# The first input projection of a two-block layer: values, gates and both z products in pairs of column chunks with seven block products in place of eight

## The reference

```python
h = rms_norm(x, norm_g)
proj = jnp.einsum('bsd,dn->bsn', h, w_in)
(q_a, k_a, v_a, o_a, i_a, f_a, z_a, c_q, c_kv, k_r, z_b, g_a, g_b) = jnp.split(proj, offsets, axis=-1)
...
y_a = jnp.einsum('bsc,cd->bsd', jax.nn.sigmoid(o_a) * h_a * jax.nn.silu(z_a), w_a)
...
y_b = jnp.einsum('bsc,cd->bsd', o_b * jax.nn.silu(z_b), w_b)
```

## Time and profile before

| | |
|---|---|
| median of 3 runs | 2136.06 us (2136.01 to 2136.29) |
| the profiled execution | 2135.79 us |
| its span, first to last instruction | 2133.6 us |
| PE busy | 2111.0 us, 99% |
| DVE busy | 1317.1 us, 62% |
| ACT busy | 1052.0 us, 49% |
| mean granted clock of PE | 0.999 of full speed |

### The profile page before, as it was taken

The page is one execution under the profiler, slowest core; times in us unless marked ns, Lnnn a source line. Parts: engine busy times, 40 slices in busy tenths (PEclk is TensorE's granted clock), DMA queues, the critical chain, the costliest instruction groups (busy, mean ns, idle before and its releaser), DMA issues.

```text
span 2133.6 us, 25857 instructions
## 1 busy us (share of the span) xinstructions
PE 2111.0 (99%) x10130; PEld 1764.8 (83%) x10130; DVE 1317.1 (62%) x1675; ACT 1052.0 (49%) x1344; POOL 37.8 (2%) x49
## 2 busy tenths in 40 slices
PE   8999999999999999999999999999999999999998
PEld 7888888888888877788888888888888888888886
DVE  5874454555555776556554455456786787687675
ACT  6445454445444675454445444354544544454443
POOL 0000000000000020000000000000000000000000
PEclk9999999999999999999999999999999999999999
DMA  7455555564465544355755442455555455555453
GB/s 268 178 191 189 193 195 197 192 227 177 174 225 197 188 152 147 135 217 197 293 187 185 180 172 103 151 185 198 182 212 194 180 199 199 189 187 215 178 197 119
DMA packets 56550, 402.44 MB, mean 189 GB/s; under 512 B 6240, under 2 KB 6496, under 8 KB 9216
## 3 DMA queue, kind: packets, MB, share of 16 engines
q1 hardware_dynamic: 53648, 380.67, 49.5%
q0 software_dynamic: 2656, 19.81, 2.4%
q10 hardware_dynamic: 144, 0.52, 0.1%
HBM read 392.59 MB, written 8.39 MB: 188 GB/s over the span
## 4 chain that ended last, share of the span: by engine, by line
PE 97%; ACT 1%; issue 1%; DVE 0%; DMA 0%; SPq 0%; POOLq 0%; POOL 0%; DVEq 0%; ACTq 0%
PE proj L554 20%; PE proj L556 20%; PE proj L555 20%; PE proj L929 11%; PE proj L932 6%; PE proj L964 2%; PE proj L965 2%; PE tbank L530 2%; PE proj L963 2%; PE tbank L963 1%; PE tbank L964 1%; PE tbank L965 1%; PE bank_a L965 1%; PE bank_a L963 1%; PE bank_a L964 1%; PE bank_a L731 1%
## 5 line engine op out<-in xcount | busy, mean ns | idle before, releaser
L1554 DVE TENSOR_TENSOR w_lo<-raw,w_hi 128x1024 fp32r<-128x1024 f32 x714 | 861.5, 1214 | 717.8 <-ACT w_hi L1092 709.5
L1092 ACT ACTIVATE w_hi<-raw 128x1024 fp32r<-128x1024 f32 x714 | 748.5, 1052 | 958.7 <-PE proj L556 663.4
L554 PE MATMUL proj<-w_hi,a_both 128*128 128x512 f32 x1728 | 686.5, 397 | 0.0
L556 PE MATMUL proj<-w_hi,a_both 128*128 128x512 f32 x1728 | 674.1, 390 | 0.0
L555 PE MATMUL proj<-w_lo,a_both 128*128 128x512 f32 x1728 | 672.7, 389 | 0.0
L556 PEld LDWEIGHTS proj<-w_hi,a_both 128*128 128x128 f32 x1728 | 324.3, 188 | 69.2
L554 PEld LDWEIGHTS proj<-w_hi,a_both 128*128 128x128 f32 x1728 | 324.5, 188 | 68.5 <-issue 4.3
L555 PEld LDWEIGHTS proj<-w_lo,a_both 128*128 128x128 f32 x1728 | 324.8, 188 | 65.1
L929 PE MATMUL proj<-a_both,w_hi 128*128 128x512 f32 x1024 | 256.5, 392 | 0.3 <-DVE a_both L1597 0.3
L929 PEld LDWEIGHTS proj<-a_both,w_hi 128*128 128x128 f32 x1024 | 184.4, 189 | 33.7 <-DVE a_both L1597 0.5
L932 PEld LDWEIGHTS proj<-a_both,w_lo 128*128 128x128 f32 x1024 | 139.7, 190 | 10.0
(11 more groups left out here) (376 smaller groups left out, 1823.1 us busy)
## 6 DMA issues: line engine op xcount, KB each, us to landing
raw<-stream SPq DMA_DIRECT2D x359, 1024.0 KB, 4.8
nat<-x SPq DMA_DIRECT2D x4, 512.0 KB, 8.2
z_store<-z POOLq DMA_DIRECT2D x1, 2048.0 KB, 8.3
ga_store<-z POOLq DMA_DIRECT2D x1, 2048.0 KB, 12.5
gb_store<-z POOLq DMA_DIRECT2D x4, 512.0 KB, 7.1
yb<-z_store POOLq DMA_DIRECT2D x4, 512.0 KB, 6.8
ga<-ga_store POOLq DMA_DIRECT2D x1, 2048.0 KB, 8.2
gb<-gb_store POOLq DMA_DIRECT2D x1, 2048.0 KB, 14.5
```

Source lines behind the costliest of these rows:

```text
L554: nc.tensor.matmul(banks[t][:, :], ah, wh, start=first, stop=False)
L556: last = nc.tensor.matmul(banks[t][:, :], al, wh, start=False, stop=end)
L1092: A((w_hi_end if extra else w_hi)[:, piece.n % RING, 0:width], src, ACT.Copy).then_inc(w_rounded, 1)
L1554: V.tensor_tensor(lo[:, s, 0:width], src, hi[:, s, 0:width].bitcast(f32), SUB).then_inc(w_rest, 1)
```

## The change

The 16 chunks of v, o, z_a and z_b become eight pairs (`PAIRS_IN`): two of v, four of one o and one z_a chunk each, two of z_b. Pairs 1 to 7 have their two sum steps where the MLP has them, pair 0 at steps 3 and 5, with the contraction tiles put in another order, so that the sums of the left side (`xs`, made once, in the k chunks, by `sum_x`, `round_x_sums` and `rest_of_x_sums`) serve all eight pairs. The mixed banks go through a buffer in SBUF, `joined`: `join_mixed` combines them after the second sum step, `join_whole` adds the whole banks at the end of the pair and leaves the finished chunks in `joined`, and what ACT and DVE do with the chunks (`take_v`, `take_o`, `take_z`) stands in the first step of the pair that follows and reads `joined`, where it read the banks. The convolution of the last k chunk, the angles of the rotation and `rope_k` are put in slots of pairs 0 and 1 (`side`). The loops are written out, on SyncE too. The helpers of the MLP's pairs are used for both.

```diff
+UNITS_IN = 1 + 4 * 4
+PAIRS_IN = 8
+SUM_AT_IN = [(3, 5)] + [SUM_AT] * (PAIRS_IN - 1)
+ORDER_IN = [(0, 2, 3, 1, 5, 4, 6, 7)] + [tuple(range(STEPS))] * (PAIRS_IN - 1)
...
+        parts_in = ([proj[2], proj[3], proj[0], proj[1]], [bank_a, bank_b] + tbank)
...
+            def pair_in(p):
+
+                whole, mixed = parts_in[p % 2], parts_in[1 - p % 2]
+                at = SUM_AT_IN[p]
+                if p:
+                    pe.wait_ge(part_read, 5 * (p - 1) + 1)
+                else:
+                    pe.wait_ge(proj_read, chunk.at() * 2)
+                for step in range(STEPS):
+                    kt = 2 * ORDER_IN[p][step]
+                    if step == at[0]:
+                        if p:
+                            pe.wait_ge(part_read, 5 * p)
+                        else:
+                            pe.wait_ge(m_sum, 1)
+                            pe.wait_ge(t_by_dve, by_dve.at())
+                    if step in at:
+                        i = at.index(step)
+                        sum_step(kt, whole, mixed, a_hi, a_lo, xs_hi[:, i], xs_lo[:, i], i + 1, i == 0, i == len(at) - 1)
...
+            def round_x_sums(i):
+
+                act.wait_ge(ms_summed, i + 1)
+                A(xs_hi[:, i, :, :], xs[:, :, :], ACT.Copy).then_inc(ms_rounded, 1)
+
+            def k_slot(j, i):
+                conv_slot(j)
+                if i in (2, 3) and j == 7:
+                    round_x_sums(i - 2)
...
+            def take_o(p, n):
+
+                act.wait_ge(whole_added, 4 * (p + 1))
+                for t in range(TT):
+                    if n == 0:
+                        act.wait_ge(gated, tiles.at(2))
+                        A(stg[:, t, :], joined[:, 2 * t, :], ACT.Sigmoid, scale=inv1[:, t:t + 1]).then_inc(proj_read, 1)
+                    else:
+                        A(stg2[:, t, :], joined[:, 2 * t + 1, :], ACT.Sigmoid, scale=inv1[:, t:t + 1]).then_inc(sig, 1)
...
+            def take_o(n):
+
+                if n == 0:
+                    return
+                i = tiles.n // 2
+                for t in range(TT):
+                    tiles.add()
+                    dve.wait_ge(sig, tiles.at())
+                    chain(V.tensor_tensor(stg2[:, t, :], stg2[:, t, :], stg[:, t, :], MUL))
+                    V.scalar_tensor_tensor(nat[:, t, i * CW:(i + 1) * CW], joined[:, 2 * t + 1, :], inv1[:, t:t + 1],
+                                           stg2[:, t, :], MUL, MUL).then_inc(gated, 1)
...
+            def join_mixed(p, part):
+
+                mixed, m = parts_in[1 - p % 2], joined
+                if part == 0:
+                    if p in (1, 2):
+                        dve.wait_ge(proj_read, chunk.at() * 2)
+                    dve.wait_ge(m_copied, p + 1)
+                    chain(V.tensor_tensor(m[:, 2, :], mixed[2][:, :], m[:, 0, :], ADD))
+                    V.tensor_tensor(m[:, 1, :], mixed[1][:, :], m[:, 2, :], ADD).then_inc(dve_seq, 1)
+                    seq.add()
+                else:
+                    chain(V.tensor_tensor(m[:, 2, :], mixed[3][:, :], m[:, 2, :], ADD))
+                    V.tensor_tensor(m[:, 3, :], mixed[1][:, :], m[:, 2, :], ADD).then_inc(part_read, 1)
...
+            def side(p, js):
+
+                if p == 0:
+                    conv_slot(js, 3)
+                    if js == 0:
+                        rest_of_x_sums(1)
+                    if js in (9, 13):
+                        if js == 9:
+                            dve.wait_ge(early_ready, 16)
+                        angles((js - 9) // 4)
+                if p == 1 and js == 6:
+                    rope_k()
+
+            def pair_in(p):
+
+                at = SUM_AT_IN[p]
+                for step in range(STEPS):
+                    def slot(j):
+                        if step in at:
+                            if j % 2 == 0:
+                                side(p, 2 * step + j // 2)
+                        else:
+                            side(p, 2 * step + j)
+                        if step == 0:
+                            take(p - 1, j)
+                        if step == at[-1] + 1:
+                            join_mixed(p, j)
+                    if step == STEPS - 1:
+                        join_whole(p)
+                    pieces(4 if step in at else 2, slot=slot)
+                chunk.add(2)
```

More of the change, by code:

```diff
@@ L655, in _, with product @@
                 project(a_hi, a_lo, slot=lambda j: stg_slot(j, i, at=(1, 3)))
[L657 to L665, removed]
+            def product(bank, hi, lo, wh, wl, first=False, end=False):
+                nc.tensor.matmul(bank[:, :], hi, wh, start=first, stop=False)
+                nc.tensor.matmul(bank[:, :], hi, wl, start=False, stop=False)
+                return nc.tensor.matmul(bank[:, :], lo, wh, start=False, stop=end)
@@ new lines, in weights, with plain_step @@
+            def weights(ahead, half):
+                s = (piece.n + ahead) % RING
+                cols = slice(half * CW, (half + 1) * CW)
+                return w_hi[:, s, cols], w_lo[:, s, cols]
+            def plain_step(kt, whole, hi, lo, first=False, slot=None):
+                for h in range(2):
+                    pe.wait_ge(w_rest, piece.at(1))
+                    for t in range(TT):
+                        tok = slice(t * P, (t + 1) * P)
+                        for n in range(2):
+                            last = product(whole[2 * t + n], hi[:, kt + h, tok], lo[:, kt + h, tok],
+                                           *weights(0, n), first=first and h == 0)
+                    last.then_inc(w_used, 1)
+                    piece.add()
+                    if slot:
+                        slot(h)
@@ L959, in project_last @@
                 chunk.add()
[L961 to L983, removed]
@@ L1189, in _, with trig_slot @@
-            act.wait_ge(proj_read, chunk.at() * 2)
-            act.sem_inc(v_ready, 8)
-            tiles = Tally()
-            with loop(act, 4, {piece: 16, done: 16, chunk: 2, tiles: 2}) as i:
-                pieces()
-                for t, b in enumerate(banks()):
+            def trig_slot(j):
+                if j == 4:
+                    act.wait_ge(trig_arg, 2)
+                    A(sin[:, :, :], sin[:, :, :], ACT.Sin).then_inc(trig, 1)
+                    A(cos[:, :, :], cos[:, :, :], ACT.Sin).then_inc(trig, 1)
@@ L1201, in _, with take @@
                 tiles.add(2)
-            with loop(act, 2, {piece: 16, done: 16, chunk: 2, tiles: 4}) as i:
-                for c in range(2):
-                    pieces()
-                    for t, b in enumerate(banks()):
-                        act.wait_ge(gated, tiles.at(2))
-                        A(stg[:, t, :], b[:, :], ACT.Sigmoid, scale=inv1[:, t:t + 1]).then_inc(sig, 1)
-                    tiles.add(2)
-            act.wait_ge(gated, tiles.at(2))
+            def take(p, n):
+                if p >= 0:
+                    (take_v if p < 2 else take_o if p < 6 else take_z)(p, n)
```

300 lines of the change are left out of this document (185 added, 115 removed).

## The result

The changed kernel takes 2153.53 us (median of 4 runs, 2150.57 to 2153.91), the kernel before 2136.03 (4 runs, 2135.67 to 2136.29): the ratio is 1.0079, with a 95% interval from 1.0062 to 1.0096. It is 17.5 us slower. The forecast was 10.8 us slower, so the sign was right, and the time lies 1.0 us above the upper end of the range, 2152.5.

The account below looks back on a forecast made before the run. The prediction took PE's count of matmuls to bound the stage. Waits of 21.8 us less 10.9 us for removed matmuls made it 10.9 us slower, stated as 2146.8 us, with a range of 2141 to 2152.5.

Parts of the forecast that it names:

- 48 matmuls less: Eight pairs, two sum steps each, 21 matmuls in place of 24: 48 x 0.2267 = 10.9 us saved on PE.
- The first wait: Start of pair 0: PE waits for ACT's reads of the last k chunk, 3.05 us, 2.5 without rounding `xs`.
- DVE in pair 0: PE waits on DVE for convolution (1.65), piece 11 (1.55), piece 16 (1.7) and `joined` (3.4), together 8.3 us.
- `take_o` at the start of pairs 3 to 6: Four DVE operations ahead of piece 6 make PE wait 2.9 us in pair 3, 2.15 in each other: 9.35 us.
- pair 7: Start of pair 7: z work behind pieces 4 and 5 on DVE makes PE wait 0.9 us (0.4 to 1.5).
- pairs 1 and 2: ACT copies v there, so piece 6 is ready later: waits of 0.1 us each.
- Nothing for the rest: k chunk sums hidden, SyncE's loads in the same order with its loop written out, same weight bytes: no cost.
- The falling clock: Rival: PE at half rate for some ten matmuls after each of three waits, 6.8 us more, 2153.5 us; chance 0.04.
- the prediction's own sum of bounds: Summed low and high waits, 17.6 and 28.0 us, giving times of 2142.7 and 2153.1 us.
- The reserve hides all: Rival: DVE's slot work runs while pieces wait, only the first wait of 3.05 us stands: 2128 us; chance 0.05.
- only pair 0 pays: Rival: `take_o` comes before piece 5 or costs under 0.8 us, waits are 11.5 us: 2136.5 us; chance 0.07.
- Weights land late: Rival: a DVE that is behind frees `raw` later, each miss costing up to 5 us; chance 0.04.

Follow-up runs that it names:

- experiment 7: Changed kernel with seven pairs, value columns 0 to 1023 as two plain chunks, results taken at step 2 of the next pair: 2126.43 us.
- experiment 2: Kernel before plus one wait: PE starts the chunk after the last k chunk only once ACT has read that chunk's banks: 2139.82 us.
- experiment 5: Kernel of experiment 4, with pair 0's step 0 for the first token tile of pieces 0 and 1 done ahead of the first wait: 2137.61 us.
- experiment 6: Kernel of experiment 4, with the rotary angles done in pair 1 in place of pair 0, their use for k in pair 2: 2134.20 us.
- experiment 8: Changed kernel, all eight pairs, with the edits of experiment 4, experiment 5 and experiment 6 together: 2131.74 us.
- experiment 9: Changed kernel unaltered, profiled again, the first of three more such executions (9 to 11), which took 2150.61, 2150.59 and 2155.32 us.
- experiment 4: Changed kernel, with each pair's results taken at step 2 of the next pair in place of step 0: 2139.68 us.
- experiment 12: Kernel of experiment 7, but with results taken at step 0 of the next pair as in the change: 2141.2 us.
- experiment 1: Kernel before with its five loops written out as straight code, nothing computed changed: 2135.84 us.

## Why the prediction was right, and why its range failed

- **48 matmuls less, 10.9 us.** Held: experiment 7 saves 42 of them, 42 x 0.2267 = 9.5 us, and measures 9.8. The Trainium skill's figure ("TensorE: Matmul & The Clock Gate", section "Back-to-back issue gap") would make it 9.1 us, an estimate; the rows were the better price here.
- **The first wait, 3.05.** Held (3.1), and its split into 2.5 and `xs` too (experiment 2).
- **DVE in pair 0, 8.3.** Held: 8.3, in the four places named, each within 0.2. Experiments 5, 6 and 8 confirm the chain: half of it goes with the angles, and the convolution's wait takes up half of what the first one gives back. The exact sum is partly luck: the waits proper were 7.9, and restarts of 0.4 in all make up the rest. The 50 us of DVE work against 43 was too much: the trace has 43.0 busy in pair 0, since two pieces and four of the eight `joined` operations fall behind the start of pair 1 (170.03 in the first execution of experiment 9). The waits were not worked out from that total.
- **`take_o` at the start of pairs 3 to 6, 9.35.** Right in mechanism and place (experiments 4 and 12), undersized by 1 us: the four operations took 3.25 where 3.2 was taken, but each wait was 0.1 longer than forecast (2.26 for 2.15), a restart costs 0.11 more each time, and pair 3 had 0.2 more a few matmuls earlier. The same holds for pair 7 (1.15 for 0.9) and pairs 1 and 2 (0.6 for 0.2). In all 1.6 us. (In pair 3's sum 6.55 - 5.7 is 0.85, not 0.75, and for the first wait 118.0 - 114.91 is 3.1, not 3.05: 0.15 us that change nothing.)
- **Nothing for the rest.** Held: written out loops cost nothing (experiment 1), weights did not land late.
- **The step that failed: "the waits here are short, so I give it little".** The falling clock stood among the rivals at 0.04, with a price of 6.8 us for three falls of ten matmuls, and in the sum it stood at nothing. No row of before gave a reason to call the waits short: the only long one there, 5.4 us at the start, told nothing either way, and the sum itself had waits of 3.05, 3.4 and 2.9 us. The runs show falls behind waits of 2.5 to 3.7 us.

  In five profiled executions of the changed kernel there were six such waits each, and 8 falls behind the 30: four of five behind the first wait, one of five each behind those at 168 and 267 us, two of fifteen behind those of 2.5. Seven to nine matmuls go at half rate (those in between the two rates counted), 1.4 to 1.7 us a time. The executions with one fall take 2150.2 to 2150.6 us at a mean clock of 0.998, that with four 2155.3 at 0.996, and the median of 2153.5 at 0.997 lies where three would put it (2150.6 + 2 x 1.6 = 2153.8). For the timed runs without a trace that is an inference from time and clock, not seen; and why they have more falls than four of the five profiled ones stays open.

  Without any fall the kernel would take some 2149 us (2150.6 - 1.6), inside the range. So of the 6.7 us between 2146.8 and 2153.5 some 4.7 are falls (by the inference just named), 1.6 restarts and small waits, and 0.4 are not assigned. That rival's number, 2153.5, came out nearly exact by luck, with the wrong factors: three falls, but of 1.6 us, and on top of waits 1.6 us larger.
- The rule it came from (the Trainium skill, the same page, section "Why this matters for your kernels") agrees with the traces in part: idle gaps between bursts of matmuls cost clock, but behind the same wait in some executions only, 8 of 30 here. Set up as all or nothing, at a chance of 0.04, the rival could not move the range. Priced wait by wait, with the numbers now known, as none to four of the six falling at 1.6 us each, it would have put 2146.8 to 2153.2 on the forecast before any other uncertainty. The range also stopped short of the prediction's own sum of bounds: it says that it takes in the bounds, but 2152.5 lies below 2153.1.
- **The other rivals.** "The reserve hides all" and "only pair 0 pays" fell. The second describes what experiment 4 made of the kernel, with 11.4 us of waits left: its fastest run took 2136.50, that rival's number, and its median 3.2 more, which is what the two falls in its profiled execution cost (1.5 and 1.6 us). "Weights land late" did not happen: no wait of PE, ACT or DVE on a transfer shows between 110 and 500 us.

## What to carry to other kernels

An engine that prepares operands for PE can stand idle and yet have no reserve: here DVE could not start on the sixth piece of a pair before PE had used an earlier one, and PE wanted the seventh ready 3.4 us after that start. Work of 3.25 us between these two pieces cost PE 2.4 us per pair; two steps later the same work was free. Look for the place with reserve before cutting work, and leave work that fills an engine (a convolution) beside the schedule with the larger reserve, even at the price of some matmuls. And price a wait of TensorE of the size seen here (2.5 to 3.7 us) with a restart and a chance of half rate behind it, not with its length alone.

## What the runs showed of the hardware

- The length of a wait alone does not decide whether the clock falls behind it: same program, same wait within 0.1 us, with a fall and without. In five executions of the changed kernel 8 of 30 waits of 2.5 to 3.7 us had one, and none of 20 of 1.2 to 2.0 us; in the profiled executions of experiments 2, 4, 5, 6, 8 and 12 it was 6 of 11 of the longer ones and none of the shorter. What decides it stayed open. The falls make scatter too: kernels without waits of 2.5 us or more from 115 to 495 us spread by 1.1 us or less (experiments 1 and 7), those with them by 1.4 to 4.4.
- Behind every wait of PE above 0.3 us at full clock the distance from the first matmul to the second was 0.30 to 0.34 in place of 0.2267; where the lower clock began with the first matmul it was 0.57 to 0.60.
